# Weight ring of eleven places, first pair in quarters of both experts, first rows gathered: a two-layer mixture-of-experts trunk

## The reference

```python
def reference(x, ...):
    h = x
    for i in range(2):
        xn = rms_norm(h, norm_mix[i])
        h = h + (sliding_window_attention(xn, ...) if i == 0 else gated_short_conv(xn, ...))
        h = h + hierarchical_moe(rms_norm(h, norm_ffn[i]), ...)
    return rms_norm(h, final_norm)

# hierarchical_moe: the best of 4 groups, in it the best 2 of 8 experts, for every token
# expert e: (silu(x @ gate_e) * (x @ up_e)) @ down_e, weighted by the token's gate and added
```

## Time and profile before

| | |
|---|---|
| median of 3 runs | 1376.79 us (1374.46 to 1380.26) |
| the profiled execution | 1375.89 us |
| its span | 1374.0 us |
| PE busy | 1299.1 us (95%) |
| DVE, ACT, POOL busy | 573.1, 256.9, 113.1 us |
| moved by DMA | 450 MB, mean 328 GB/s |

### The profile page before, as it was taken

The page is one execution under the profiler, slowest core; times in us unless marked ns, Lnnn a source line. Parts: engine busy times, 40 slices in busy tenths (PEclk is TensorE's granted clock), DMA queues, the critical chain, the costliest instruction groups (busy, mean ns, idle before and its releaser), DMA issues.

```text
span 1374.0 us, 14898 instructions
## 1 busy us (share of the span) xinstructions
PE 1299.1 (95%) x6082; PEld 721.4 (53%) x6082; DVE 573.1 (42%) x1234; ACT 256.9 (19%) x556; POOL 113.1 (8%) x120
## 2 busy tenths in 40 slices
PE   7999998999999998999989999989999999998996
PEld 5777673444444443444678888734444444443442
DVE  5576332433334333343566661323443334333334
ACT  3267511000100110000532221110000100101002
POOL 3950000000000000000000000000000000000001
PEclk9999999999999999999999999999999999999998
DMA  9302667999999999999533336469999999999993
GB/s 348 88 1 85 269 260 312 429 427 427 426 427 427 426 426 426 428 427 424 155 101 110 121 155 270 199 261 410 426 427 426 426 426 427 427 426 426 427 426 150
DMA packets 65020, 450.11 MB, mean 328 GB/s; under 512 B 17592, under 2 KB 32978, under 8 KB 40372
## 3 DMA queue, kind: packets, MB, share of 16 engines
q1 hardware_dynamic: 58976, 436.09, 76.8%
q0 software_dynamic: 5472, 11.95, 2.2%
q10 hardware_dynamic: 500, 1.06, 0.2%
HBM read 450.74 MB, written 6.32 MB: 333 GB/s over the span
## 4 chain that ended last, share of the span: by engine, by line
PE 89%; DVE 3%; issue 3%; ACT 2%; DMA 2%; SPq 0%; POOLq 0%; DVEq 0%
PE ps L1184 32%; PE ps L950 19%; PE ps L1209 17%; PE ps L1176 9%; PE ps L1134 2%; PE ps L1144 2%; DMA arena<-h_rows,arena 2%; PE ps L1092 1%; PE ps L1031 1%; PE ps L1127 1%; PE ps L1170 1%; ACT arena L802 1%; PE ps L998 1%; PE ps L1202 1%; PE ps L1018 1%
## 5 line engine op out<-in xcount | busy, mean ns | idle before, releaser
L1184 PE MATMUL ps<-big,arena 128*64 128x512 f32 x1200 | 458.6, 595 | 16.0 <-issue 16.0
L1184 PEld LDWEIGHTS ps<-big,arena 128*64 128x64 f32 x1200 | 139.6, 137 | 151.3 <-issue 151.0
L1777 DVE TENSOR_TENSOR h<-ps,h 128x512 f32<-128x512 f32 x240 | 148.9, 683 | 95.5 <-PE ps L1176 95.5
L1209 PE MATMUL ps<-small,arena 128*64 128x512 f32 x336 | 149.4, 598 | 3.3 <-ACT arena L802 3.1
L1184 PE MATMUL ps<-small,arena 128*64 128x512 f32 x336 | 150.4, 595 | 1.3 <-issue 1.3
L1176 PE MATMUL ps<-arena_parts 128*128 128x512 f32 x512 | 134.7, 405 | 1.7 <-DVE arena_parts L1737 1.7
L1737 DVE SCALAR_TENSOR_TENSOR arena_parts<-ps,slot_gate,arena_parts 128x512 fp32r<-128x512 f32 x64 | 48.0, 750 | 211.1 <-ACT arena_parts L811 211.1
L1176 PEld LDWEIGHTS ps<-arena_parts 128*128 128x128 f32 x512 | 91.2, 188 | 52.4 <-issue 35.1
L950 PE MATMUL ps<-xt_parts,small_parts 128*128 128x512 f32 x288 | 112.3, 399 | 5.4 <-DVE big_parts L1671 3.5
L797 ACT ACTIVATE gain<-ps,slot_root 128x512 f32<-128x512 f32 x32 | 22.0, 687 | 510.1 <-PE ps L1184 510.1
L950 PE MATMUL ps<-xr_parts,small_parts 128*128 128x512 f32 x272 | 107.3, 395 | 0.0
(11 more groups left out here) (213 smaller groups left out, 1689.4 us busy)
## 6 DMA issues: line engine op xcount, KB each, us to landing
big<-in_moe_w_gate_up_dram SPq DMA_DIRECT2D x75, 2048.0 KB, 24.5
small<-in_moe_w_gate_up_dram SPq DMA_DIRECT2D x21, 2048.0 KB, 24.2
small<-in_moe_w_down_dram SPq DMA_DIRECT2D x21, 2048.0 KB, 26.3
arena<-in_moe_w_gate_up_dram SPq DMA_DIRECT2D x11, 2048.0 KB, 22.5
xr<-in_moe_w_down_dram SPq DMA_DIRECT2D x11, 2048.0 KB, 25.8
xt<-in_moe_w_down_dram SPq DMA_DIRECT2D x11, 2048.0 KB, 24.2
arena<-in_moe_w_down_dram SPq DMA_DIRECT2D x11, 2048.0 KB, 26.4
xr<-in_moe_w_gate_up_dram SPq DMA_DIRECT2D x11, 2048.0 KB, 22.4
```

What stands on the lines that cost most here:

```text
L1184: mm = nc.tensor.matmul(ps[2 + half][j * BLOCK:(j + 1) * BLOCK, :], xg[:, k, j * BLOCK:(j + 1) * BLOCK], ws[j][:, k % FT, half * FF:(half ...
L1209: mm = nc.tensor.matmul(ps[6 + c][j * BLOCK:(j + 1) * BLOCK, :], hidT[:, k, j * BLOCK:(j + 1) * BLOCK], ws[j][:, k, c * HALF:(c + 1) * HAL ...
L1777: ins = V.tensor_tensor(hs, ps[bank + c][:], hs, ALU.add)
```

## The change

The ring has eleven places. The room comes from three sides: the kernel is built with a scratch of 2048 bytes per partition for the descriptors of POOL's DMAs, where the builder's default stood before; some small buffers share memory (`rt` lies over `y_high` and `y_low`, `sel` over `hidT`, `ones` is a broadcast column, the eye of `spread` lies in `upper`, which POOL builds anew for layer 1); and `tab` has 8 columns in place of 68, since it holds a token's first expert and its two gates, not a gate for each expert.

The first four pieces of a layer are quarters of gate_up (two of the eight k) of both experts; each is freed when its quarter has been multiplied. The first pair's rows are gathered as all others are: PE computes its indexes ahead of its gate_up, then two matmuls that only keep it busy, and waits for the gather. In every pair the tiles 3 and 2 are combined behind the second half of gate_up, the hidden rows are transposed before the next pair's rows, and those go to other banks of PSUM. ACT's silu is written in the transposed order straight into `hid`. At the end POOL scales tile 0 of the output alone, by gain and by root, and DVE the other three.

```diff
-    RING = 9
+    RING = 11
...
+        rt = arena[:, at_y:at_y + TT * 256].rearrange("p (t n) -> p t n", t=TT)
         tab = cut(TT, TAB)
-        over_tab = cut(TT, 8)
-        pair_eye = cut(2, P)
         where = cut(AHEAD).bitcast(I32)
+        wide = cut(FT, D)
...
-        ring = [[halves[1][0], small[:, 0], late_slot, halves[1][1], xr[:], xt_slot, halves[0][1], halves[0][0], small[:, 1]],
-                [*halves[1], xr[:], halves[0][0], late_slot, small[:, 1], halves[0][1], small[:, 0], xt_slot]]
+        ring = [[wide, late[:, 1], halves[1][0], small[:, 0], late[:, 0], halves[1][1], xr[:], xt_slot, halves[0][1], halves[0][0],
+                 small[:, 1]],
+                [wide, *halves[1], xr[:], halves[0][0], late[:, 0], small[:, 1], halves[0][1], small[:, 0], late[:, 1], xt_slot]]
...
-                early = [(0, (mix_ps, 2 * TT)), (1, (mix_ps, 2 * TT)), (6, (pT_ps, 4 * 6)), (7, (score_ps, 2 * U)),
-                         (2, (score_ready, HG * U)), (3, (mix_ps, 4 * TT)), (4, (mix_ps, 4 * TT)),
-                         (5, (logits_ps, TT)), (8, (mix_ps, 4 * TT))] if l == 0 else \
-                    list(enumerate([(gates_ps, DT)] * 3 + [(half_ps, 1)] * 3 + [(mix_ps, 6 * TT)] * 2 + [(logits_ps, 2 * TT)]))
+                early = [(2, (mix_ps, 2 * TT)), (0, (mix_ps, 2 * TT)), (3, (mix_ps, 2 * TT)), (8, (pT_ps, 4 * 6)),
+                         (9, (score_ps, 2 * U)), (4, (score_ready, HG * U)), (1, (pT_ps, 4 * U)), (5, (mix_ps, 4 * TT)),
+                         (6, (mix_ps, 4 * TT)), (10, (mix_ps, 4 * TT)), (7, (logits_ps, TT))] if l == 0 else \
+                    list(enumerate([(gates_ps, DT)] * 4 + [(half_ps, 1)] * 3 + [(mix_ps, 6 * TT)] * 3 + [(logits_ps, 2 * TT)]))
 
                 def load(n):
                     i, c = divmod(n, PIECES)
+                    if c < 4 and i == 0:
+                        w = w_gate_up[l, 0:2].rearrange("e (p k) n -> p e k n", p=P)[:, :, 2 * c:2 * c + 2]
+                        sp.dma_start(both_experts(ring[l][n]), w).then_inc(ring_in[n], 16)
+                        return
...
-                        sp.wait_ge(main.gu_done, 2 * (l * PAIRS + before) + used // 2 + 1)
+                        sp.wait_ge(main.gu_done, ups_before(l, before) + (used // 2 if before else used) + 1)
...
+                    gather(S, l, n, i % AHEAD, 2 * n if i else None)
                     if i:
-                        gather(S, l, n, i % AHEAD, 2 * n)
-                    else:
-                        pool.wait_ge(S.index_ready, n + 1)
-                    if n >= 2:
-                        pool.wait_ge(S.spread, n - 1)
-                    nc.gpsimd.tensor_copy(parts(pair_eye[0:E, i % 2, :].rearrange("p (j s) -> p j s", j=2)),
+                        pool.wait_ge(S.spread, n)
...
+            pool.wait_ge(h_ready, 2 * (TT + 1))
+            nc.gpsimd.tensor_tensor(xr[:, 0, :], h[:, 0, :], gain[:], ALU.mult).then_inc(pool_scaled, 1)
+            pool.wait_ge(pool_scaled, 1)
+            pool.wait_ge(scale_ready, 1)
+            nc.gpsimd.tensor_scalar(xr[:, 0, :], xr[:, 0, :], rstd[:, 0:1], None, ALU.mult).then_inc(pool_scaled, 1)
...
-            def pick_first(S, l):
-
-                pe.wait_ge(first_selected, l + 1)
-                for k in range(DT):
-                    for t in range(TT):
-                        mm = nc.tensor.matmul(ps[k // 4][:, k % 4 * P:(k % 4 + 1) * P],
...
-            def first_indexes(S, l):
-
-                o = l * PAIRS
-                pe.wait_ge(S.selected, o + 1)
-                pe.wait_ge(tab_ready, l + 1)
-                index(S)
-                turn_ranks()
-                count(l)
-                pe.wait_ge(S.selected, o + 2)
-                index(S)
-                pe.wait_ge(ranks_taken, l + 1)
...
+                pe.wait_ge(S.selected, o + 1)
+                index(S, 0, GATE)
+                count(l)
+                turn_ranks()
+                pe.wait_ge(tab_ready, l + 1)
+                index(S, GATE, TAB)
+                pe.wait_ge(S.selected, o + 2)
+                index(S)
+                keep_busy(2, 3)
+                pe.wait_ge(S.picked_in, 16 * (o + 1))
+                turn_picked(S, 0)
...
-                    ws = weights(i, 0)
                     pe.wait_ge(S.rows_taken, 2 * n + 1)
-                    gate_up(both((0, 1, 2, 3)), ws).then_inc(S.gu_done, 1)
+                    if i:
+                        pe.wait_ge(S.rows_taken, 2 * n + 2)
+                        ws = weights(i, 0)
+                        gate_up(both((0, 1, 2, 3)), ws).then_inc(S.gu_done, 1)
+                    else:
+                        for c in range(2):
+                            ws = quarter(c)
+                            gate_up(both((2 * c, 2 * c + 1)), ws, 2).then_inc(S.gu_done, 1)
                     if i == 0:
-                        first_indexes(S, l)
+                        pe.wait_ge(ranks_taken, l + 1)
                     spread(S, n, i)
                     if i:
-                        add_tiles(i - 1, (0, 1))
-                    ws = weights(i, 2)
-                    pe.wait_ge(S.rows_taken, 2 * n + 2)
-                    gate_up(both((4, 5)), ws)
+                        pe.wait_ge(S.y_ready, 2 * n)
+                        pe.wait_ge(S.selT_ready, n)
+                        pe.wait_ge(S.added, l * ADDS + TT * (i - 1))
+                        add_tile(i - 1, 0, 0)
+                        add_tile(i - 1, 1, 6)
                     if i:
-                        add_tiles(i - 1, (2, 3))
-                    last_quarter(S, ws)
-                    if i < LAST:
-                        if i:
-                            pe.wait_ge(S.added, l * ADDS + TT * (i - 1) + 3)
-                        pe.wait_ge(S.picked_in, 16 * (l * LAST + i + 1))
-                        turn_picked(S)
+                        ws = weights(i, 2)
+                        gate_up(both((4, 5)), ws)
+                        last_quarter(S, ws)
+                    else:
+                        pe.wait_ge(S.rows_taken, 2 * n + 2)
+                        ws = quarter(2)
+                        gate_up(both((4, 5)), ws, 2).then_inc(S.gu_done, 1)
+                        last_quarter(S, quarter(3), 2)
+                    if i:
+                        pe.wait_ge(S.added, l * ADDS + TT * (i - 1) + 2)
+                        add_tile(i - 1, 3, 6)
+                        add_tile(i - 1, 2, 0)
                     if i + 2 < PAIRS:
                         pe.wait_ge(S.selected, n + 3)
                         index(S)
                     pe.wait_ge(S.selT_ready, n + 1)
+                    turn_hidden(S, n)
+                    if i < LAST:
+                        pe.wait_ge(S.picked_in, 16 * (n + 2))
+                        turn_picked(S, 2)
+                    ws = weights(i, 4)
                     if i:
-                        pe.wait_ge(S.added, l * ADDS + TT * i)
+                        pe.wait_ge(S.added, l * ADDS + TT * (i - 1) + 3)
                     else:
                         pe.wait_ge(route_ready, l + 1)
-                    turn_hidden(S, n)
-                    ws = weights(i, 4)
                     down(S, n, ws)
...
-                V.tensor_tensor(first_sel.rearrange("p t (j s) -> p t j s", j=2),
...
+                dve.wait_ge(main.indexed, l * INDEXES + 1)
+                find_index(main, 0)
+                find_root(main, 0)
+                for n, gate in enumerate((gate1, gate2)):
+                    at = GATE + 2 * n
+                    step(V.tensor_copy(parts(tab[:, :, at]), gate[:]))
+                    ins = V.tensor_tensor(parts(tab[:, :, at + 1]), gate[:], parts(tab[:, :, at]), ALU.subtract)
+                ins.then_inc(tab_ready, 1)
...
+                    hidden(S, n, ups_before(l, i + 1), i % AHEAD)
                     if i:
-                        add_tile(i - 1, 2, 0)
-                        add_tile(i - 1, 3, 6)
-                    hidden(S, n, i % AHEAD)
+                        add_tile(i - 1, 2, 3, 6)
+                        add_tile(i - 1, 3, 2, 0)
...
+    nc = _bacc.Bacc("TRN2", target_bir_lowering=False, num_devices=1, dynamic_dma_scratch_size=2048)
```

More of the change, by code:

```diff
@@ L83, in build_trunk @@
         rounded = {k: sb(k + "_parts", shape, F32R) for k, shape in shared.items()}
-        big, small, xr, xt, arena = (plain[k] for k in shared)
+        big, small, xr, xt, arena, upper, gain = (plain[k] for k in shared)
         h = sb("h", [P, TT, D])
-        gain = sb("gain", [P, D])
         ident = sb("ident", [P, P])
-        upper = sb("upper", [P, P])
-        ones = sb("ones", [P, P])
+        single = sb("single", [P, 8])
+        one, base, slot_id, eps, warm = (single[:, k:k + 1] for k in range(5))
+        ones = one[:].to_broadcast([P, P])
         iota = sb("iota", [P, BLOCK])
-        base = sb("base", [P, TT])
         wr = sb("wr", [P, DT, NR])
@@ L551, in _ @@
```

(23 more changed lines are left out.)

237 lines of the change are left out of this document (116 added, 121 removed).

## The result

| | before | after |
|---|---|---|
| median of 4 runs, us | 1378.43 (1374.46 to 1380.26) | 1337.03 (1334.29 to 1337.23) |
| the profiled execution, its span | 1375.89, 1374.0 | 1337.05, 1335.1 |
| mean granted clock | 0.987 | 0.976 |

The changed kernel takes 0.9699 of the time before, interval 0.9672 to 0.9726. The span fell by 38.9 us. I forecast 1330, within 1321 to 1343. The forecast gain of 47.1 is 8.2 more than that of the span.

A forecast was written before the change was run, and what follows sets the result against it. PE and the weight stream were taken to run nearly level in the experts, DMA the bound at the end. Terms 10.6 + 13.8 + 20.4 + 1.6 + 0.7 = 47.1 us gave about 1330; own range 1322 to 1338, widened to 1321 to 1343.

The forecast's parts named there:

- A: Start of each layer's first gate_up: a gather replaces picking the first rows; 5.3 us gained each, 10.6 in all.
- B: Pair 0 up to pair 1: index products moved, wait for pair 1's gather gone; 6.0 and 7.8 us gained, 13.8.
- C: Pair 1 to piece 91: eleven places leave 77 pieces between, not 79; 10.2 us a layer gained, 20.4.
- rival 1: First gather lands late: A gains 1.8 in place of 10.6 and clock is lost; about 1341 us, chance 0.11.
- the clock loss I leave as it is: Step in B: clock loss in pair 0 stays unchanged; up to 3.6 us more gain if keep-busy products hold it.
- DMA ends last by very little: Step in C: PE's 14 pairs take 383.6 to 390.9 us, still below the stream's 391.7.
- D: Last pair of each layer: two combined tiles fill part of PE's 1.87 us wait; 0.8 a layer gained, 1.6.
- E: The end, output scaling: POOL takes tile 0, DVE three of 1.28 us; 0.7 us gained, between nothing and 2.2.
- D full: Case in the range's lower end: D at its full bound, 1.87 us each, entered as 0.5 us below.
- The signs I named: First gate_up 5 us earlier, gather about 7; pair 0 25 and 26 us; few late weight waits; gathers still 10.5.

The follow-up runs named there:

- e1: The changed kernel with nine ring places in place of eleven and the early list of before; 1352.87 us, ratio 0.9842.
- e0: The changed kernel itself once more, run beside e6, e7 and e8 on the same chip; 1334.39 us, ratio 0.9685.
- e3: The changed kernel with the output scaled as before: POOL multiplies tiles 0 and 1 by gain, DVE scales them; 1334.11 us, ratio 0.9707.
- e8: The changed kernel with pair 0's gate_up in whole halves of one expert, not quarters; 1339.89 us, ratio 0.9717.
- e6: The changed kernel with more unread keep-busy products before the first gather lands and before the last pair's weights; 1332.94 us, ratio 0.9665.
- e7: e6 and e3 together on the changed kernel, plus ACT's silu table loaded early by a dummy activation; 1330.07 us, ratio 0.9652.
- e2: The changed kernel with tiles 2 and 3 combined mid second half and DVE's hidden product after its additions, as before; 1341.36 us, ratio 0.9758.
- e5: The changed kernel with three of six pieces a pair, from pair 1 on, loading only 128 KB; one run, 1306.01 us beside 1378.05 for before.
- e4: The kernel before with only the descriptor scratch of 2048 bytes; 1378.23 us, ratio 1.0015.

## Why the prediction was nearly right, step by step

**One figure explains A, B and C together.** Take the time from the first load that waits for the experts to the start of the last pair, in us:

| | pieces between | layer 0 | layer 1 |
|---|---|---|---|
| before | 83 | 210.5 to 636.5: 426.0 | 900.5 to 1329.5: 429.0 |
| e1, nine places | 83 | 205.3 to 628.7: 423.4 | 881.7 to 1304.8: 423.1 |
| after | 81 | 204.8 to 619.0: 414.2 | 875.1 to 1288.3: 413.2 |
| e0, after again | 81 | 202.8 to 616.0: 413.2 | 872.4 to 1285.7: 413.4 |
| e3, old tail | 81 | 204.4 to 617.9: 413.5 | 874.1 to 1287.9: 413.8 |
| e8, no quarters | 81 | 207.7 to 620.5: 412.8 | 880.0 to 1292.6: 412.6 |
| e6, clock held | 81 | 203.1 to 616.4: 413.3 | 871.6 to 1286.0: 414.4 |
| e7 | 81 | 203.6 to 619.0: 415.4 | 872.2 to 1285.6: 413.4 |

81 pieces at 5.09 are 412.3, 83 are 422.5. All these kernels with eleven places lie within 3.2 us of that, nine of the twelve layers within 1.5, whatever pair 0 took (24.0 to 27.1 us). Only e2, where PE is the bound, has 416.3 and 416.4. Before had 3.5 and 6.5 more: four pieces from 210.49 end at 210.49 + 4 x 5.09 = 230.9, and the next load came at 234.66. The shorter pair 0 closed that hole. So the gain of layer 0, 636.53 - 619.01 = 17.5, is 5.7 by the earlier release and 11.8 by two pieces and less of a hole. B, as a stretch of its own, is only worth what it does to these.

**A** (10.6 forecast, 10.0 measured) came nearly as worked out. The landings of 7.35 and 6.20 us stand for the 7.0 taken, so rival 1 is out. From the landing to gate_up it took 2.0 us where I had 1.4: the eight transposes took 1.97 us for 1.09 in the earlier trace rows, at a granted clock of 0.50.

**B** (13.8, 12.4) is right in layer 1 and 1.9 short in layer 0. The step that failed: "the clock loss I leave as it is, since PE will stand for about 3 us before the gather lands too". It did stand so (2.8 us), but the loss moved and grew. Before, it fell on pair 0's down (the chain of before, 7.09 at full clock):

```profile
226.56 8.06 PE ps L1209 x32
```

Now it lies ahead of the first release, which came 204.83 - 198.97 = 5.9 us after gate_up's start in layer 0, where I had 3.5, and 4.6 in layer 1. Where the clock held (e6), pair 0 took 24.8 us in both layers, for the 25.2 and 26.3 that I had. ACT's table load of 1.28 us and the silu behind it are exposed too, which I had not counted; by e7 the table load costs pair 0 0.4 to 0.8 us and the whole nothing that can be seen.

**C** (20.4, 18.9) is right in its mechanism, by e1 and e5. The 1.2 us that layer 0 lacks in this execution are 0.5 in e0. What failed beside it is "DMA ends last by very little": PE's pair fell to 27.2 us, below the 27.4 to 27.92 that I allowed, so PE alone would be 12 to 13 us a layer shorter than the stream, not 0 to 8.

**D** (1.6, -0.7) has the wrong sign. The order brought what I said where the clock held: 27.0 us in e0 and e6 for the 28.1 of before. But a longer wait stands before the last pair, 2.1 us for 1.3, and its first half took 8.78 us for 7.09 in the earlier trace rows, with 0.68 of the clock in the window. I left the clock out of this term. In e6, where products fill that wait, the grant is 1.00 and the half takes 7.09 us. That the longer wait brings the clock down is argued, not shown: in the traces of after, e0, e1, e3 and e8 every slow last pair (five) stands behind 2.1 us, and the four behind 0.9 us or less were not slow, but one in e3 stands behind 2.1 us and was not slow either.

**E** (0.7, -1.9) has the wrong sign. I priced POOL's unseen second operation only by what it takes off DVE. It takes 3.91 us itself, and the four stores, issued one behind the other in 2.88 us, begin only when it ends. In e3 they begin while DVE still scales:

```profile
1319.19 4.70 POOL L663 TENSOR_TENSOR xr<-h,gain 128x1024 f32<-128x1024 f32 x2 [52.97 <-DVE h L1772]
...
1324.46 3.98 SPq L545 DMA_DIRECT2D out_dram<-xr  x4
```

An estimate from the products, 2.35 us each, would end it at 1326.6 and not at 1328.2. The Trainium skill (SBUF — State Buffer, "Who interferes with whom") has DVE and GpSimd share one port pair that one instruction holds at a time. The trace agrees only in part: of DVE's three scalings the one that lies wholly beside POOL's took 1.95 us and the last 1.28, but the first, which started 0.1 us ahead of it, took 1.28 too with POOL beside it nearly all the time. No run here tells how much of the 3.91 us is the operation's own and how much DVE's presence.

**The total.** No errors cancelled: each of the five terms came out below its forecast, D and E even with the wrong sign, and together they are 8.4 us short, with 0.2 back between the layers. 1337 lies at the upper end of the forecast's own range, to 1338. The lower end had a slip: "D full" adds 2.1 us by the bounds that I gave, not 0.5.

**The signs I named.** Gate_up came 4.5 and 5.5 us earlier in its layer, behind gathers of 7.35 and 6.20 us, and the wait at the transposes of pair 1's rows is gone. Three others failed. Pair 0 of layer 0 took 27.1 us, not 25. The waits for weights are 19.1 us in 13 waits over five pairs, not a few us in two or three. And the gathers' median rose from 10.5 to 11.2 us, which I had named a sign of being wrong. It is not the scratch alone (10.5 in e4) and not the two places (11.1 in e1). No wait stands behind these gathers in after, so it cost nothing here; its cause is open.

That the shorter pair brings nothing of its own was forecast and is shown by e1: its C is that of before. The bandwidth of 426 GB/s held, 5.10 us a piece over 81 (413.2 us in after's layer 1); an estimate by the 358 GB/s of the Trainium skill (SBUF — State Buffer, "Summary: rules for kernel authors") does not fit any row here.

## What to carry to other kernels

Where a stream of weights and an engine run nearly level, count from the first release to the last piece: pieces times time per piece, plus holes. Places in the ring and an earlier first release are then worth their full time, and work saved on the engine only keeps it from becoming the bound. Look for a short standstill just ahead of that release, because slow matmuls there put it off; here, though, holding the clock in all these places (e6) was worth 1.4 us at the median, which the intervals don't tell from nothing. And price an operation that is handed to another engine by its own duration first.

## What the runs showed of the hardware

- Short waits of PE for weights and the clock, in the traces of after, e0, e1, e3, e6, e7 and e8: behind 32 waits of 2.1 to 2.5 us the next 32 matmuls took 7.1 us in 18 cases and 8.7 to 8.8 in 14; behind the ten of 3.2 to 3.9 us they always took 8.7 to 9.9. In the middle of the stretch such a loss only shortens later waits; in the last pair it is paid.
- ACT's silu of 128x512 takes 1158 ns where it writes in transposed order, 687 before. The rows of the two pages, after and before:

```profile
L814 ACT ACTIVATE gain<-ps,slot_root 128x512 f32<-128x512 f32 x32 | 37.0, 1158 | 449.4 <-PE ps L1180 449.3
```
```profile
L797 ACT ACTIVATE gain<-ps,slot_root 128x512 f32<-128x512 f32 x32 | 22.0, 687 | 510.1 <-PE ps L1184 510.1
```

- POOL's TENSOR_SCALAR on 128x1024 float32 took 3.91 us beside DVE's scalings, its TENSOR_TENSOR of the same shape 2.38.
- A gather lands in 4.0 us at the median beside a stream of some 260 GB/s (e5) and in 11.2 beside 426 (after); in the kernel before, the smaller descriptor scratch left the median at 10.5 (e4).
